# Projections as single fp32 products instead of three products of split halves

## The reference

```
h  = rmsnorm(x, gain)
z  = h @ w_in                       # the layer's input projections, 1024 wide contraction
o  = mixer(z, state or paged cache)
x  = x + (o * silu(g)) @ w_out      # the output projection, 1024 x 1024
```

## Time and profile before

| | |
|---|---|
| Time, median of 3 runs | 1154.49 us (1151.8 to 1155.49) |
| Span of the profiled execution, first to last instruction | 1153.2 us |
| PE busy, share of the span, instructions | 1115.8 us, 97%, 10579 |
| PEld busy | 976.9 us, 85% |
| DVE busy | 674.4 us, 58% |
| ACT busy | 494.4 us, 43% |
| POOL busy | 382.5 us, 33% |
| Moved by DMA | 168.81 MB, mean 146 GB/s |
| Granted TensorE clock, mean | 0.996 of full speed |

### The profile page before, as it was taken

How to read it: one execution, slowest core, us unless ns; L and a number is a source line. 1 busy time by engine, 2 the same in 40 slices (tenths; PEclk the granted TensorE clock), 3 DMA queues, 4 the chain that set the end, 5 groups by cost and what they waited for, 6 DMA issues and landing times. The chain is left out here.

```text
span 1153.2 us, 25599 instructions
## 1 busy us (share of the span) xinstructions
PE 1115.8 (97%) x10579; PEld 976.9 (85%) x10579; DVE 674.4 (58%) x1215; ACT 494.4 (43%) x968; POOL 382.5 (33%) x321
## 2 busy tenths in 40 slices
PE   8999999899999999999999999999999999999897
PEld 6889888799758988888955599999999889888796
DVE  6462255764999779776444555595444362255742
ACT  6542466643443322222254554322453451467643
POOL 5534313234313423114300044353344245312230
PEclk9999999999999999999999999999999999999999
DMA  5235233333314787884779932233220335233202
GB/s 174 96 110 165 87 116 111 129 82 100 112 56 151 237 280 237 273 308 138 256 285 409 377 116 91 66 101 127 83 74 3 111 107 163 78 128 111 97 33 78
DMA packets 127788, 168.81 MB, mean 146 GB/s; under 512 B 20385, under 2 KB 93481, under 8 KB 127664
## 3 DMA queue, kind: packets, MB, share of 16 engines
q1 hardware_dynamic: 115609, 152.59, 39.6%
q10 hardware_dynamic: 12062, 14.59, 3.6%
HBM read 150.70 MB, written 16.81 MB: 145 GB/s over the span
## 5 line engine op out<-in xcount | busy, mean ns | idle before, releaser
L737 POOL TENSOR_TENSOR w_lo<-raw,w_hi 128x512 fp32r<-128x512 f32 (+2 forms) x267 | 359.9, 1380 | 691.4 <-ACT w_hi L1501 691.4
L773 PE MATMUL psum<-h_hi,w_hi 128*128 128x272 f32 x1616 | 471.2, 292 | 6.6 <-DVE h_lo L2425 4.7
L775 PE MATMUL psum<-h_hi,w_lo 128*128 128x272 f32 x1616 | 467.3, 289 | 0.0
L774 PE MATMUL psum<-h_lo,w_hi 128*128 128x272 f32 x1616 | 464.9, 288 | 0.0
L773 PEld LDWEIGHTS psum<-h_hi,w_hi 128*128 128x128 f32 x1616 | 303.3, 188 | 20.2 <-issue 15.3
L774 PEld LDWEIGHTS psum<-h_lo,w_hi 128*128 128x128 f32 x1616 | 303.7, 188 | 0.1
L775 PEld LDWEIGHTS psum<-h_hi,w_lo 128*128 128x128 f32 x1616 | 303.0, 187 | 0.0
L1501 ACT ACTIVATE w_hi<-raw 128x1024 fp32r<-128x1024 f32 (+1 forms) x137 | 135.5, 1034 | 118.5 <-PE psum L775 81.0
L773 PE MATMUL psum<-w_hi,h_hi 128*128 128x512 f32 (+2 forms) x352 | 125.6, 357 | 1.4 <-DVE dsa_score_s L2519 0.8
L775 PE MATMUL psum<-w_hi,h_lo 128*128 128x512 f32 (+2 forms) x352 | 122.5, 348 | 2.3 <-issue 2.3
L774 PE MATMUL psum<-w_lo,h_hi 128*128 128x512 f32 (+2 forms) x352 | 122.5, 348 | 0.7 <-issue 0.7
(11 more groups left out here) (331 smaller groups left out, 1367.3 us busy)
## 6 DMA issues: line engine op xcount, KB each, us to landing
smp_keys<-in_cache_k_dram SPq DMA_DIRECT2D x128, 256.0 KB, 4.7
raw<-in_gla_w_in_dram SPq DMA_DIRECT2D x23, 1024.0 KB, 5.3
raw<-in_dsa_w_in_dram SPq DMA_DIRECT2D x17, 1024.0 KB, 5.3
spare<-in_cache_v_dram SPq DMA_DIRECT2D x34, 512.0 KB, 8.3
raw<-in_cache_v_dram SPq DMA_DIRECT2D x30, 512.0 KB, 8.6
gla_s_in<-in_state_gla_dram SPq DMA_DIRECT2D x16, 512.0 KB, 7.8
raw<-in_gla_w_out_dram SPq DMA_DIRECT2D x8, 1024.0 KB, 6.7
out_dram<-gla_s_in ACTq DMA_DIRECT2D x16, 512.0 KB, 4.6
```

The costliest lines, as they stand in the source:

```text
L737: pool.tensor_tensor(copies(key, pair_view(w_lo, key)[:, k]), raw_copies(key, k), copies(key, pair_view(w_hi, key)[:, k].bitcast(F32)), AL ...
L773: pe.matmul(out, lh, rh, start=start, stop=False)
L774: pe.matmul(out, lh, rl, start=False, stop=False)
L775: return pe.matmul(out, ll, rh, start=False, stop=stop)
```

## The change

All projections become one fp32 matmul from the landed weights and unsplit inputs. The type fp32r is no longer used.

- `product`, `split_in`, `pair_view` and the pairs `w_hi`, `w_lo` go; `raw` has seven buffers instead of three, the same memory in all. TensorE waits for a block's landing (`loaded`), and SP for the last product of the block that had the buffer before.
- ScalarE's `split_hi`, `first_split`, `out_hi`, and VectorE's `first_lo`, `input_lo`'s subtraction, `out_lo`, `low` go; GpSimd's subtractions go. The inputs have one tile per pair (`H[n]`), written at once by the engine that wrote the temporary or the high part: VectorE for the first layer's input and the branches, ScalarE for the later layers' inputs.
- The decode rows of v and k read the same tile (`h[:, k, SEQ:TOK]`); the separate `h_s` goes.
- The rank-16 weights are repeated to 128 columns by one ScalarE copy at the head of each GLA layer (`copy_a`).
- The decode queries' bands get a tile of their own in what was the low part's room; the order of DSA's weight items against its key pages is computed for seven buffers.

```diff
-RAW, SPARE = 3, 4
-PAGES = RAW + SPARE
-QSLOT = 2
+RING = 7
+PAGES = RING
...
-            H.append((sb(f"h{n}_hi", [P, KT, TOK], F32R), sb(f"h{n}_lo", [P, KT, TOK], F32R)))
-        pair_end = [pair_at[1], place["at"]]
-        raw = sb("raw", [P, RAW, 2048])
-        w_hi = sb("w_hi", [P, 2, 2048], F32R)
-        w_lo = sb("w_lo", [P, 2, 2048], F32R)
...
+            H.append(sb(f"h{n}", [P, KT, TOK]))
+            place["at"] += size([P, KT, TOK], F32)
+            pair_end.append(place["at"])
+        raw = sb("raw", [P, RING, 2048])
...
-                order = [(starts[n - 3] + 2 if n > 2 else 4 * n - 12, FILL[f][0:2]) for n, f in enumerate(starts)]
+                order = [(max(starts[n - RING + 1] if n >= RING else -20, f - 14), FILL[f][0:2])
+                         for n, f in enumerate(starts)]
...
                     if items[index[old]][4] != "w":
                         sp.wait_ge(*on("pages_used", old))
-                    elif s < RAW and by_rows(old):
-                        sp.wait_ge(*on("proj", ("item", old)))
-                    elif s < RAW:
-                        sp.wait_ge(*on("split", old))
                     else:
-
                         sp.wait_ge(*on("proj", ("item", old)))
...
-            def product(out, lh, ll, rh, rl, start, stop):
-                pe.matmul(out, lh, rh, start=start, stop=False)
-                pe.matmul(out, lh, rl, start=False, stop=False)
-                return pe.matmul(out, ll, rh, start=False, stop=stop)
+            def loaded(key):
+
+                pe.wait_ge(*on(landed(slot[key]), key))
...
-                        mm = product(psum[0:m, b, 0:HC], *lhs(k), *rhs(k, c), k == 0, k == kk - 1)
+                        mm = pe.matmul(psum[0:m, b, 0:HC], lhs(k), rhs(k, c), start=k == 0, stop=k == kk - 1)
...
+            def copy_a(L):
+
+                key = (L, "a")
+                act.wait_ge(*on(landed(slot[key]), key))
+                copy(a_copies(key).rearrange("p k (c n) -> p k c n", n=RANK),
+                     raw_view(key).unsqueeze(2).broadcast_to([P, KT, P // RANK, RANK])).then_inc(*sig("a_copies", L))
...
-                for x, k in enumerate(pieces(key)):
-                    pool.wait_ge(*on("split_hi", key, x * 2 // len(pieces(key)) if n else ("k", x)))
-                    pool.tensor_tensor(copies(key, pair_view(w_lo, key)[:, k]), raw_copies(key, k),
-                                       copies(key, pair_view(w_hi, key)[:, k].bitcast(F32)), ALU.subtract)\
-                        .then_inc(*sig("split", key, x, also=((key,),) if k.stop == items[index[key]][2] else ()))
...
-                    hi, lo = H[L % 2]
-                    dve.wait_ge(*on("h_hi", (L, "in"), m, part))
-                    dve.scalar_tensor_tensor(out=lo[:, m, c], in0=XT[:, m, c], scalar=gains[:, L, m:m + 1],
-                                             in1=hi[:, m, c].bitcast(F32), op0=ALU.mult, op1=ALU.subtract)\
-                        .then_inc(*sig("h_lo", (L, "in"), m, part))
...
-                    dve.tensor_tensor(tmp.rearrange("p (k t) -> p k t", k=4), src.rearrange("p (k t) -> p k t", k=4),
-                                      gate_g[:, 4 * half:4 * half + 4, cols(t)], ALU.mult)\
-                        .then_inc(*sig("oT_read", L, t, half))
...
+                    dve.tensor_tensor(h[:, k, cols(t)], src.rearrange("p (k t) -> p k t", k=4),
+                                      gate_g[:, k, cols(t)], ALU.mult).then_inc(*sig("h", (L, "out"), t, half))
```

More of the change, by code:

```diff
@@ L373, in program, with free_from @@
         index = {it[0]: n for n, it in enumerate(items)}
[L374 to L392, removed]
-        for n, it in enumerate(items):
[L395 to L402, removed]
+        slot, before, held_by = {}, {}, {s: None for s in range(PAGES + 4)}
+        dsa_at = KINDS.index(1)
+        def free_from(s):
+            return -1 if held_by[s] is None else index[held_by[s]]
+        for n, it in enumerate(items):
+            key, choice = it[0], list(range(RING))
             if it[4] == "K":
                 choice = [PAGES + 2 * PAIR_AREA[key[2] // 2] + key[2] % 2]
-                if key[2] == 0:
-                    bands_after, held_by[QSLOT] = held_by[QSLOT], (key[0], "K", 4 * NPAGE - 1)
-            s = min(choice, key=lambda x: free_from(x, values[0]))
+            s = min(choice, key=free_from)
             slot[key], before[key], held_by[s] = s, held_by[s], key
-        last_spare = [[k for k in values if slot[k] in spares_of((first_out + x) % 2)][-1] for x in range(2)]
         def held(s):
@@ L422, in raw_view, with a_copies, branch_done @@
             return held(slot[key])[:, 0:kk * w].rearrange("p (k n) -> p k n", k=kk)
[L424 to L436, removed]
+        def a_copies(key):
+            return held(slot[key])[:, 1024:2048].rearrange("p (k n) -> p k n", k=KT)
         def band(j):
             return slice(j * NS, (j + 1) * NS)
[L441 to L449, removed]
+        def branch_done(eng, L):
+            if KINDS[L] == 1:
+                eng.wait_ge(*on("os_read", L, 1, 1))
+                eng.wait_ge(*on("h", (L, "out"), *QUADS[-1]))
+            elif KINDS[L] == 0:
+                eng.wait_ge(*on("h", (L, "out"), SMP, 1))
+            else:
+                eng.wait_ge(*on("h", L, "y", KT - 1))
         def blocks(L):
@@ L982, in first @@
                             last_bank.append(last_squares(L + 1, "rest"))
-                        if new:
-                            split_in(key, k)
+                        if new and k == 0:
+                            loaded(key)
                         if ask:
@@ L1270, in project @@
                     key = (L, name, i)
-                    wh, wl = pair_view(w_hi, key), pair_view(w_lo, key)
-                    if x == 0 and name != "q":
-                        pe.wait_ge(*on("split", key))
+                    w = raw_view(key)
+                    if x == 0:
+                        loaded(key)
                     if name == "v":
                         b = claim(next_bank(range(2)), ("proj", key, x), ("v_d", key, x))
-                        hi, lo = H[L % 2]
                         for k in range(KT):
-                            mm = product(psum[0:rows(x), b, 0:HALF], hi[:, k, cols(x)], lo[:, k, cols(x)],
-                                         wh[:, k, :], wl[:, k, :], k == 0, k == KT - 1)
+                            mm = pe.matmul(psum[0:rows(x), b, 0:HALF], H[L % 2][:, k, cols(x)], w[:, k, :],
+                                           start=k == 0, stop=k == KT - 1)
                         mm.then_inc(*sig("proj", (key, x), also=((("item", key),),) if x == TILES - 1 else ()))
@@ L1611, in rstd_rows @@
                 act.wait_ge(*on("rstd_tok", L))
-            def out_hi(L, t, half, tmp):
-                act.wait_ge(*on("oT_read", L, t, half))
-                n, k = rows(t), slice(0, KT) if t == SMP else slice(4 * half, 4 * half + 4)
-                copy(H[L % 2][0][:, k, cols(t)],
-                     tmp[:, 0:(k.stop - k.start) * n].rearrange("p (k t) -> p k t", k=k.stop - k.start))\
-                    .then_inc(*sig("h_hi", (L, "out"), t, half))
             def f_out(name, out, mark, fn=ACT.Copy, sample=None, parts=(0, 1)):
@@ L2403, in gla, with gated @@
                 sequence(DB - 1)
[L2405 removed]
+                def gated(t, half):
                     dve.wait_ge(*on("oT", L, t, half))
@@ L2447, in gla @@
-                low(5)
+                    k = slice(4 * half, 4 * half + 4)
+                    dve.tensor_tensor(h[:, k, cols(t)], src.rearrange("p (k t) -> p k t", k=4),
+                                      gate_g[:, k, cols(t)], ALU.mult).then_inc(*sig("h", (L, "out"), t, half))
+                for t, half in OUT_PIECES[0:2]:
+                    gated(t, half)
+                gate_part(15)
+                for t, half in OUT_PIECES[2:6]:
+                    gated(t, half)
                 out_rows(SMP)
@@ L2451, in gla @@
                 normalise(SMP)
-                piece(6)
-                piece(7)
-                low(6)
-                piece(8)
-                low(7)
-                low(8)
+                for t, half in OUT_PIECES[6:]:
+                    gated(t, half)
                 resid(L)
             def dsa(L):
-                decode_input(L)
                 for s in range(3):
```

416 lines of the change are left out of this document (113 added, 303 removed).

## The result

The changed kernel takes 1312.08 us, the median of three runs (1311.3 to 1312.12), against 1154.49 before: 1.1378 times as long, with an interval of 1.135 to 1.1405. The forecast was 1311. The profiled execution has a span of 1309.6 us, 156.4 more than the 1153.2 before, and a mean granted clock of 0.998.

What follows compares the result with a forecast made beforehand. TensorE was taken as the bound almost everywhere: 175.1 us more for products, less 12 for switching kinds and 7 for splitting waits, makes 156 us on the 1153.2 span; with 1.3 around it, 1311 us, range 1280 to 1338.

Steps and rivals of the forecast that it cites:

- The bound: Whole kernel: TensorE is the bound almost everywhere, matmuls busy 97% of the span, so a product's price counts in full.
- The price of a product: Projections on TensorE: one fp32 matmul costs more than three split-half matmuls, 0.459 against 0.378 us at 272 columns; 175.1 us more.
- Rival 2: Projections: one record is a whole fp32 product, so products get cheaper; 320 us less, 834 us; chance 2%.
- Switching kinds: TensorE, between fp32 groups and halves' matmuls: late starts at 82 entries disappear, giving back 12 us.
- no step of 0.1 over the rule: Sign, between the attention's matmuls and the projections: no start 0.1 us later than the usual step remains.
- Waits for splitting: TensorE's waits for low parts and a late decode state, 11.0 us together: 7 us given back, bounds 0 and 11.
- Seven landing buffers: Weight loads: landings of 5.3 us hide behind items of 14.7 us; cost 0, upper end 42 us.
- Rival 3: Landing buffers make TensorE wait, one late landing at each of eight stage boundaries: 42 us on top, 1353 us; chance 8%.
- Rival 1: Sparse-attention layer: its products only fill holes, so 45 us of the price are not seen; 1266 us; chance 10%.
- GpSimd, ScalarE, VectorE emptied: Sign, other engines: GpSimd nearly idle, ScalarE and VectorE each lower, and none of that in the span.
- waits for DMA below 5 us: Sign, TensorE in the changed kernel: its waits for DMA should stay below 5 us.
- The range: Total time: whole range 1280 to 1338 us, said to reach half-way to rivals 1 and 3; forecast's own 1295 to 1332.

Runs made afterwards that it cites:

- the first experiment: The kernel before with all its splitting, waits and buffers, but each product one fp32 matmul of the high parts; 1320.83 us, ratio 1.146.

## Why the prediction was right, step by step

- **The bound.** Right: a price on TensorE counted nearly in full upwards (156 of 176 us here, 256 of 271 with a fourth matmul). It would not have held downwards (138 of 271).
- **The price of a product.** Right to 1 us in 175. The fp32 matmuls that the kernel already had (lines 814, 1113, 1374) were the sample, and the distance of starts was the measure; the mean ns of one in the earlier trace rows would have misled, since it puts three halves (3 x 292 ns) above two fp32 records (2 x 392) where the truth is 0.378 against 0.459. Rival 2, one record a product, is rejected by the 3296 records, two a product and 0.229 apart. The Trainium skill's "FP8 and Floating Point Precision", section TensorE Precision Notes, counts four passes for true FP32, the low-by-low one among them. The trace agrees with it roughly: the fp32 matmul's 0.458 us are 3.6 steps of the halves' 0.126, and the kernel with four separate matmuls was 88 us slower than the one with a single fp32 matmul.
- **Switching kinds, 12 us given back.** Wrong: this step of the sum failed, and so did the sign that no step of 0.1 over the rule would be left between the attention's matmuls and the projections. The changed kernel has no halves' matmuls, and still the late steps stand at most of these places, as large as before. Before, the group that begins at 130.15 in the earlier trace rows is followed by

```profile
132.89 0.39 PE L773 MATMUL psum<-h_hi,w_hi 128*128 128x272 f32 x1
133.12 0.29 PE L774 MATMUL psum<-h_lo,w_hi 128*128 128x272 f32 x1
```

  and after, the same group stands between (the records on either side are shown singly)

```profile
150.58 0.39 PE L796 MATMUL psum<-h,raw 128*128 128x272 f32 x1
150.90 0.27 PE L1083 MATMUL psum<-gla_q,gla_k 128*32 128x32 f32 x8
...
153.65 0.50 PE L796 MATMUL psum<-h,raw 128*128 128x272 f32 x1
153.98 0.39 PE L796 MATMUL psum<-h,raw 128*128 128x272 f32 x1
```

  The group starts 0.32 behind the projection ahead of it and the second projection 0.33 behind the first, 0.09 and 0.10 over the rule of 0.229; before it was 0.22 and 0.23 over 0.126, the same excess. From the last projection ahead of the group to the second behind it is 3.19 us before (from 129.93) and 3.40 after; less two steps of each kernel's own, 0.252 and 0.458, that is 2.94 in both. Counted in the same way from the records, 37 of the 46 groups between projections of 272 columns agree to 0.02 us, and in each of the other nine TensorE waited before for another engine or a DMA. So the excess was put down to the wrong cause, and nothing of it came back.
- **Waits for splitting, 7 us.** Right within its bounds of 0 to 11: by the first experiment, taking the splitting away and adding the buffers is worth 9 us (4 to 15). What the sum did not have is the waits that the longer matmuls cover by themselves, some 10 us in the same experiment, the decode state's 2.4 among them, which I had put down to the splitting's buffers. They stand in the place of the 12 us for switching. That the two are nearly equal, so that 19 us taken back met 20, is luck.
- **Seven landing buffers, 0.** Right, but by less margin than I argued. With five buffers TensorE still waits for no weight block, but 7.0 us for value pages, and the price is some 9 us. Rival 3 had the mechanism and a wrong place (stage boundaries).
- **Rival 1, the attention layer absorbs its share.** Rejected: the layer grew by 51 us. The rival's 45 us was itself too low a count: the layer's output projection (128 products of 272 columns, 10.4 us) and the indexer's 16 (1.3) belong to it, 57 in all. It gave back 6 of these, of the 20 us that the whole kernel gave back.
- **GpSimd, ScalarE, VectorE emptied, nothing of it in the span.** Right but for the waits above: 360 us less on GpSimd, 9 us of time by the first experiment.
- **The sign "waits for DMA below 5 us".** Missed as worded: they sum to 6.5 us, 6.1 of them the two at the head, which were there before (5.4). Behind weight or value buffers it is 0.4.
- **The range.** Half-way from its upper end, 1332, to rival 3 is 1342, not 1338; the result does not depend on it.

## What to carry to other kernels

Price a change of matmul kind by the distance of starts of the same kind and width somewhere in the trace, times the count, and check whether TensorE has idle time that would absorb it. Here three matmuls of split halves beat one fp32 matmul (0.378 against 0.459 us for 272 columns, 1154 against 1312 us in all), with the splitting done beside them on other engines; four lose (1409 us). Emptying engines that nobody waits for returned some 9 us of time for 360 us of GpSimd's work. Work taken off TensorE pays in part only once its waits begin, because of the waits themselves and of the clock that falls with them. An unexplained small step in a timeline should be looked for in the other kernel too, before a price is given to its cause.

## What the hardware showed that was not expected

- Behind a group of other matmuls the first record of a stream can start ahead of its work and last longer by as much: 0.49 us against 0.29 behind an fp32 pair among halves, where the sum of the steps shows that nothing is lost. In the changed kernel, without halves, a first record has 0.50 against 0.39; whether time is lost there no run tells. Only the distance over a whole group is a time.
- The clock adds to what waits cost: with two matmuls a product, 79 us of new idle time came with 44 us of longer busy time (mean clock 0.946); with one in layers 2 and 3 and part of layer 1 the mean was 0.925. The changed kernel, with TensorE busy for 98% of the span, had 0.998.
- The granted clock of a stretch can differ between executions of the same code: 0.97 and 1.00 at 50 to 100 us and at 500 to 550 us.
